# PEER gate matrix on one core: second-key one-hots moved from VectorE and ScalarE to GpSimd, and the first u rows gathered from the middle of the build

## The reference, cut to what matters

```python
expert = idx1 * PEER_KEYS + idx2
gate = jax.nn.softmax(c_top, axis=-1)
...
u = u_table[eb]
hid = jax.nn.gelu(jnp.einsum('td,thkd->thk', xb, u)) * gb
return jnp.einsum('thk,thkd->td', hid, v_table[eb])
```

## Time and profile before

| what | value |
|---|---|
| median of three runs | 3613.68 us |
| profiled execution | 3616.06 us |
| its span | 3614.3 us |
| TensorE busy | 3446.2 us, 95% of the span |
| VectorE busy | 2816.2 us, 78% |
| ScalarE busy | 1078.7 us, 30% |
| GpSimd busy | 1424.3 us, 39% |
| mean granted TensorE clock | 0.982 of full |

### The profile page before, as it was taken

The page is one execution under the profiler, slowest core; times in us unless marked ns, Lnnn a source line. Parts: engine busy times, 40 slices in busy tenths (PEclk is TensorE's granted clock), DMA queues, the critical chain, the costliest instruction groups (busy, mean ns, idle before and its releaser), DMA issues.

```text
span 3614.3 us, 39996 instructions
## 1 busy us (share of the span) xinstructions
PE 3446.2 (95%) x11593; PEld 1976.7 (55%) x11593; DVE 2816.2 (78%) x6484; ACT 1078.7 (30%) x2721; POOL 1424.3 (39%) x1233
## 2 busy tenths in 40 slices
PE   7999989999997999768899999999999999999998
PEld 4666667777774566556444444444444444444443
DVE  2466686777774489899788888987888888888898
ACT  3233344444442222277221112111211122121212
POOL 1000000000001277400566565655565566655665
PEclk9999999999997999889999999999999999999999
DMA  3111012000002234247999999999999999999998
GB/s 112 30 36 35 0 50 91 23 23 29 29 35 114 50 70 80 34 136 208 396 392 375 394 382 393 378 379 355 395 373 382 389 399 376 375 394 377 388 377 328
DMA packets 313936, 829.65 MB, mean 230 GB/s; under 512 B 41504, under 2 KB 145056, under 8 KB 305056
## 3 DMA queue, kind: packets, MB, share of 16 engines
q0 software_dynamic: 165888, 537.01, 40.1%
q1 hardware_dynamic: 125104, 227.45, 17.4%
q10 hardware_dynamic: 22768, 63.18, 4.5%
HBM read 789.73 MB, written 37.81 MB: 229 GB/s over the span
## 4 chain that ended last, share of the span: by engine, by line
PE 49%; issue 4%; DVE 2%; DMA 1%; POOL 0%; ACT 0%; ACTq 0%; DVEq 0%; POOLq 0%
PE peer_ps_o L1958 24%; PE peer_ps_d L1945 22%; PE peer_ps_q L1886 2%; DMA peer_vr<-in_v_rows,peer_index 1%; DVE peer_mt L2133 0%; DVE peer_mt L2137 0%; DMA peer_ur<-in_u_rows,peer_index 0%; PE peer_ps_s L1896 0%; DVE Y L2173 0%; POOL peer_ur L1854 0%; POOL peer_vr L1861 0%; DVE peer_ur L2162 0%; PE peer_ps_o L1926 0%; DVE route_hit L1221 0%; DVE peer_chosen L1223 0%
## 5 line engine op out<-in xcount | busy, mean ns | idle before, releaser
L1854 POOL DMA_INDIRECT peer_ur<-in_u_rows,peer_index x512 | 568.9, 1111 | 608.9 <-DVE peer_ur L2162 401.6
L2173 DVE SCALAR_TENSOR_TENSOR Y<-peer_vr,osq,Y 128x1024 f32<-128x1024 f32 x512 | 657.0, 1283 | 90.4 <-DMA peer_vr<-in_v_rows,peer_index 88.2
L1861 POOL DMA_INDIRECT peer_vr<-in_v_rows,peer_index x512 | 585.7, 1144 | 321.6 <-issue 152.4
L2162 DVE SCALAR_TENSOR_TENSOR peer_ur<-peer_ur,Y 128x1024 f32<-128x1024 f32 x512 | 628.0, 1227 | 7.8 <-DMA peer_ur<-in_u_rows,peer_index 7.5
L1945 PE MATMUL peer_ps_d<-hnT,route_ut 128*128 128x512 f32 x1376 | 598.5, 592 | 0.0
L1958 PE MATMUL peer_ps_o<-hw,Y 128*128 128x512 f32 x1024 | 448.3, 598 | 12.8 <-DVE Y L2149 12.8
L1958 PE MATMUL peer_ps_o<-hnT,Y 128*128 128x512 f32 x1024 | 442.6, 592 | 0.0
L1945 PEld LDWEIGHTS peer_ps_d<-hnT,route_ut 128*128 128x128 f32 x1376 | 261.3, 190 | 327.7 <-issue 327.7
L1958 PEld LDWEIGHTS peer_ps_o<-hw,Y 128*128 128x128 f32 x1024 | 196.2, 192 | 255.8 <-issue 239.1
L1958 PEld LDWEIGHTS peer_ps_o<-hnT,Y 128*128 128x128 f32 x1024 | 193.5, 190 | 238.2 <-issue 238.2
L1945 PE MATMUL peer_ps_d<-hnT,peer_ut 128*128 128x512 f32 x672 | 295.2, 592 | 0.0
(11 more groups left out here) (331 smaller groups left out, 4945.9 us busy)
## 6 DMA issues: line engine op xcount, KB each, us to landing
route_ut<-in_u_cols SPq DMA_DIRECT2D x86, 512.0 KB
hw<-in_v_cols SPq DMA_DIRECT2D x16, 2048.0 KB
peer_mt<-sel ACTq DMA_DIRECT2D x64, 512.0 KB
hnT<-in_v_cols SPq DMA_DIRECT2D x16, 2048.0 KB
peer_ut<-in_u_cols SPq DMA_DIRECT2D x42, 512.0 KB
route_wk<-in_w_route ACTq DMA_DIRECT2D x14, 1024.0 KB
hnT<-in_w_route SPq DMA_DIRECT2D x9, 1024.0 KB
route_wk<-in_w_route SPq DMA_DIRECT2D x9, 1024.0 KB
```

The source lines that it names most:

```text
L1854: pool.indirect_dma_start(ur[:, r % RING, :], None, u_rows, bass.IndirectOffsetOnAxis(ap=index[:, r // TOPK % 4, r % TOPK:r % TOPK + 1], a ...
L1861: pool.indirect_dma_start(vr[:, r % RING, :], None, v_rows, bass.IndirectOffsetOnAxis(ap=index[:, r // TOPK % 4, r % TOPK:r % TOPK + 1], a ...
L2162: nc.vector.scalar_tensor_tensor(out=ur[:, s, :], in0=ur[:, s, :], scalar=1.0, in1=Y[:, b, D:MIX], op0=ALU.mult, op1=ALU.mult, accum_out=d ...
L2173: nc.vector.scalar_tensor_tensor(out=hb, in0=vr[:, s, :], scalar=hid[:, c:c + 1], in1=hb, op0=ALU.mult, op1=ALU.add).then_inc(comb_done, 1)
```

## The change

GpSimd gets a new function `hot_rest(j)`, which makes three of the four `hot_b` of a group with the instruction that VectorE used. VectorE makes one (`DVE_HOT = 1`), ScalarE none: `hot_last` goes, and with it the negated plane of `pickedT` and its copy. TensorE waits for `hot_rest_ready` in place of `last_ready`. GpSimd runs through all 96 groups and issues the five first gathers of u rows after its part of group 30 (`U_ROWS_AT`).

```diff
-        pickedT = sb("pickedT", [P, 2, 4, P])
+        pickedT = sb("pickedT", [P, 2, 3, P])
...
+        DVE_HOT = 1
+        U_ROWS_AT = 30
...
         def _(pool):
+            def hot_rest(j):
+                b, t = j // (P // 4), j % (P // 4) * 4
+                pool.wait_ge(pick_out, b + 1)
+                need(pool, sel_made, j - 1)
+                for q in range(DVE_HOT, 4):
+                    ins = nc.gpsimd.tensor_scalar(hot_b[j % 2][:, q, :], R.count[:],
+                                                  pickedT[:, b % 2, 1, t + q:t + q + 1],
+                                                  pickedT[:, b % 2, 2, t + q:t + q + 1], ALU.is_equal, ALU.mult)
+                ins.then_inc(hot_rest_ready, 1)
...
-            for r in range(RING):
-                u_row(r)
+            for j in range(M_GROUPS):
+                hot_rest(j)
+                if j == U_ROWS_AT:
+                    for r in range(RING):
+                        u_row(r)
             pool.wait_ge(sel_out[3], sel_stores(3))
...
-                pe.wait_ge(last_ready, j + 1)
+                pe.wait_ge(hot_rest_ready, j + 1)
...
-                nc.scalar.activation(pickedT[:, b % 2, 0:3], ps_t[:, 0:3, :], ACT.Copy)
-                nc.scalar.activation(pickedT[:, b % 2, 3], ps_t[:, 2, :], ACT.Copy, scale=-1.0).then_inc(pick_out, 1)
-
-            def hot_last(j):
...
+                nc.scalar.activation(pickedT[:, b % 2], ps_t[:, 0:3, :], ACT.Copy).then_inc(pick_out, 1)
...
-            hot_last(0)
-            hot_last(1)
...
-                if j + 2 < M_GROUPS:
-                    hot_last(j + 2)
...
-                for q in range(3):
+                for q in range(DVE_HOT):
                     ins = nc.vector.tensor_scalar(hot_b[j % 2][:, q, :], R.count[:], pickedT[:, b % 2, 1, t + q:t + q + 1],
                                                   pickedT[:, b % 2, 2, t + q:t + q + 1], ALU.is_equal, ALU.mult)
```

More of the change, by code:

```diff
@@ L1747, in peer @@
         hot_a_ready, hot_b_ready, sel_made, staged = sem("hot_a_ready"), sem("hot_b_ready"), sem("sel_made"), sem("staged")
-        last_apart, last_ready = sem("last_apart"), sem("last_ready")
+        hot_rest_ready = sem("hot_rest_ready")
         sel_out = [sem(f"sel_out{i}") for i in range(4)]
```

## The result

The changed kernel takes 3751.47 us (median of four, 3742.87 to 3757.13); the kernel before, measured beside it, 3613.93 (four runs). The ratio is **1.0379** (95% interval 1.0359 to 1.0399): 137.5 us slower, where +10 was forecast and +41 was the top of the range. The direction was right; the size was off thirteenfold.

The account below looks back on a forecast made before the run. VectorE was taken to bound the build at 1.40 us a group, GpSimd after the change at 1.45. Beat +4.8, gathers +6.5 and routing -1.0 gave +10.3 us: 3624 us, range 3595 to 3655.

Parts of the forecast that it names:

- What bounds it: Build: VectorE bounds it at 1.40 us per group; the change touches nothing in the full dense loop, which only shifts.
- Part one: Build: VectorE loses 0.54 us per group, ScalarE 0.39 + 0.49; TensorE would bound next, winning at most 26 us.
- Part two: Build: GpSimd's three new one-hot instructions take 0.34 us each, 1.02 us per group; ends 0.78 and 1.26.
- my sum: Build beat +4.8 us, gathers +6.5, routing -1.0: +10.3 us in all.
- Part three: Build: GpSimd and VectorE exclude each other at the SBUF ports, 0.56 + 0.10 - 0.23 us per group; beat 1.45.
- my sign for it: Build: VectorE's wide one-hot lengthened from 0.69 to 1.0 us or more by waiting for the ports.
- each waits for the other: Shared ports: GpSimd and VectorE both wait, then pay only their streaming parts, 0.89 of 1.04 and 0.29 of 0.42 us.
- it is GpSimd that never waits: Build: VectorE runs a group ahead and waits, so GpSimd works without pause, its ports contested in every group.
- Part four: Five gathers after GpSimd's group 30: TensorE starves 7.0 us, 1.0 comes back, its low clock adds 0.5; sum +6.5 us.
- Part five: Routing after group 24: GpSimd makes two groups ahead while TensorE idles some 9 us, -1.0 us.
- Rival 3: Build: GpSimd's instruction costs like a two-input one, or locks change hands with a loss: 3647 to 3685 us; chance 0.20.
- The sign: Whole kernel: slower, +10.3 us; chance of slower 0.52, of faster 0.28.

Follow-up runs that it names:

- both experiments on it: Changed kernel without VectorE's wide one-hot from the third group on: 3709.15 us; changed kernel with the wide one-hot's key numbers read from PSUM: 3710.48 us.
- the last variants: Kernel before with one one-hot on GpSimd, key numbers in PSUM, gathers spread; VectorE makes the last one-hot every fourth group, or ScalarE always: 3611.05 and 3611.40 us.
- the best division tried: Kernel before with one one-hot per group on GpSimd, key numbers in PSUM, spread gathers, last one-hot ScalarE's mostly or always: 3611.05 and 3611.40 us, build 145.2.

## Why the prediction was wrong in size and right in sign

**What bounds it** held: the build alone moved, and nothing in the dense loop.

**Part one** (what goes) held: VectorE fell to 15.65 of 50 us and ScalarE to 11.00. What they were relieved of was worth nothing, since neither bounded any more.

**Part two** is the step that failed. "I take the middle, 0.34 us", ends 0.26 and 0.42, measured 0.787. The upper end was drawn from an operation with two tensor inputs, in the belief that what an instruction reads sets its price. The runs show three other terms: 0.29 for stream and arithmetic (as the select), 0.35 for a comparison as the first operation, 0.15 for the two scalars. They add up in this order of taking away; the run with the comparison alone (0.597) suggests, by the estimate of 0.12 us there, that the second operation's share depends on what stands before it. I had even said that no such instruction is in the trace; then a neighbour's price is no upper end, and the range should have gone on to what a price of twice that makes. (0.787 - 0.34) x 288 = 129 us, which is about the whole error: 137.5 - 10.3 = 127. With the measured price my sum gives 3 x 0.787 + 0.43 = 2.79 us a group, so 96 x 1.39 + 5.5 = +139 us. That it comes so near to 137.5 is in part luck, since the errors of the other parts have both signs (below). The sentence on the Trainium skill's GPSIMD Engine Reference (Engine selection: one-input work roughly line-rate) is borne out by the multiplications, 0.293 us, and not by the comparison, 3.3 ns an element.

**Part three** (the ports) held in kind and nearly in size. I had 0.56 + 0.10 - 0.23 = 0.43 us a group; the trace has 3 x 0.174 = 0.52, of which the wide one-hot makes 3 x (0.961 - 0.808) = 0.46. The rule of the Trainium skill's SBUF — State Buffer (Who interferes with whom), two SBUF inputs against GpSimd's reads, agrees with both experiments on it, 42 and 41 us. That the lock is exclusive for a whole instruction is not what the trace of the changed kernel shows: in six groups the wide one-hot started 0.26 to 0.29 us into a GpSimd instruction, this one kept 0.79 and the wide one-hot 0.69 to 0.72, and only the next GpSimd instruction was longer (0.96). But my sign for it, a wide one-hot of 1.0 us or more, did not appear. Of "each waits for the other" only one half came: GpSimd paid, and VectorE kept 0.69 even where GpSimd's instruction had started 0.11 us before. That both are released by the same semaphore, and VectorE starts 0.07 us sooner, is therefore not the whole reason; why GpSimd yields stays open.

The run with multiplications tests the rest of the sum, for there the instruction is 0.293, inside my ends. By my working: 0.88 + 0.43 = 1.31 us a group, -9 us, +5.5 for parts four and five: 3.5 us faster. Measured: 9.4 slower, 13 us more. GpSimd was busy for 124.3 us, 1.29 a group, near the 1.31 that I had; but "it is GpSimd that never waits" is wrong there. Apart from the routing's pause it waited 22.2 - 9.3 = 12.9 us for TensorE: with two buffers, and 1.13 us of products against 1.29 of one-hots, handing over between the engines is not free. This is a second step that failed, hidden in the changed kernel, where the dear instruction leaves TensorE time.

**Part four** held: five gathers, 1643.65 to 1650.23, 6.6 us where 7.0 was said, a hole of 7.19 in TensorE.

**Part five** was too small. GpSimd did run ahead, and in the changed kernel TensorE's pause for the routing is 5.66 us, where it was 9.28; GpSimd itself stands still for only 4.15:

```profile
1629.92 3.76 PE L1941 MATMUL peer_ps_o<-peer_mt 128*128 128x128 f32 x16 [5.66 <-DVE peer_mt L2136]
...
1632.14 3.88 POOL L1858 TENSOR_SCALAR peer_mt<-route_count,peer_pickedT 128x128 f32<-128x128 f32 x4 [4.15 <-PE peer_ps_o L1941]
```

That is nearer to -4 than to the -1.0 of my sum. It was not tested by a run of its own.

**Rival 3** named the right mechanism, a dear instruction, with too small a price (3647 at 0.42 us, 3685 at its far end); it had a chance of 0.20 and the range stopped half-way into it.

**The sign** was right, but partly by luck: it hung on 0.05 us a group, and with the lower end of part two the same sum says faster. The run with multiplications came out slower where that sum says faster.

What stays open: the changed kernel's spread of 14 us between executions, where the kernel before has 1 to 5, why the wide one-hot is not held by a GpSimd instruction already under way, and what made the last variants 4 us faster.

## What to carry to other kernels

An operation that the trace doesn't show on an engine has no upper bound from its neighbours there: measure it alone, at its real shape and with its real operators, before work is moved to that engine. Two multiplications and a comparison with a multiplication look alike in the code and cost 0.29 and 0.64 us here. And before an engine is eased, look whether a second one stands right behind it: here VectorE and ScalarE were both at 1.4 us, and the best division tried made the build 2 us shorter.

## What the runs showed of the hardware that was not expected

- On GpSimd a tensor_scalar of 128 x 128 fp32 takes 0.293 us with two multiplications, 0.641 with comparison and multiplication, 0.787 with two per-partition scalars in place of the constants. VectorE does the last in a pitch of 0.27.
- Reading one operand from PSUM left VectorE's tensor_tensor at 0.692 us and took away its hold on GpSimd (mean 0.961 to 0.808, 41 us of the kernel).
- Which of the two engines waits was not a matter of who started first: with GpSimd's instruction 0.11 us ahead, it took 1.30 us and VectorE's wide one-hot 0.69 (19 groups of 96 in the changed kernel).
- TensorE's granted clock was 0.53 to 0.57 in the changed build (1.2 GHz most of the time), where its products waited 106.9/96 = 1.1 us in the mean before each group; a group took 2.04 us in place of 1.13. It cost little here: GpSimd waited for TensorE 9.9 us in all, 4.15 of them in the routing's pause.
